# Gated delta-rule decoder step: row spreads and the samples' outer product as one-pass fp32r matmuls with the high and low parts stacked in contraction rows

## What is computed

```python
z = h @ w_in
b_raw, a_raw = z[..., -16:-8], z[..., -8:]                # one value per token and head
beta = sigmoid(b_raw)
g = -exp(a_log) * softplus(a_raw + dt_bias)
o, s_new = _gated_delta_chunked(q, k, v, g, beta, s0)
...
gc = cumsum(chunks(g), axis=-1)
decay = where(tril, exp(gc[..., :, None] - gc[..., None, :]), 0)
lmat = where(strict, einsum('nbhid,nbhjd->nbhij', k * beta, k) * decay, 0)
tinv = triangular_solve(eye + lmat, eye)
u, w = tinv @ (v * beta), tinv @ (k * beta * exp(gc))
# per chunk
v_new = u - w @ s
o = (q * exp(gc)) @ s + (q @ k.T * decay) @ v_new
s = s * exp(gc[-1]) + (k * exp(gc[-1] - gc)).T @ v_new
```

## Time and profile before

| what | value |
|---|---|
| time, median of 3 runs | 1707.37 us (all: 1711.52, 1707.2, 1707.37) |
| span of the profiled execution | 1703.2 us (the page gives no other time of it; it lies 4.2 us under the median) |
| TensorE matmul busy | 1613.1 us, 95% |
| TensorE weight load busy | 1518.8 us, 89% |
| VectorE busy | 850.8 us, 50% |
| ScalarE busy | 515.6 us, 30% |
| GpSimd busy | 219.7 us, 13% |
| mean granted TensorE clock | 0.916 of full |

### The profile page before, as it was taken

One profiled execution on the slowest core, in us unless ns is written; L12 is line 12 of the kernel. 1 busy time (PEld: TensorE's weight loads), 2 busy tenths in 40 slices (PEclk: granted clock), 3 DMA queues, 4 the chain that ended last, 5 costly groups with the idle time before them and its releaser, 6 DMA issues.

```text
span 1703.2 us, 30528 instructions
## 1 busy us (share of the span) xinstructions
PE 1613.1 (95%) x11944; PEld 1518.8 (89%) x11944; DVE 850.8 (50%) x1268; ACT 515.6 (30%) x783; POOL 219.7 (13%) x183
## 2 busy tenths in 40 slices
PE   6999999999999999979999999998879999999998
PEld 5995588999999999978998889887769999999997
DVE  5445512544344334666667666765435443443343
ACT  4122112332122222433343344333224221221234
POOL 5410000200000000213212321231112000000002
PEclk8995555999999999989999999997579999999999
DMA  5345200464355322312122122110022332332322
GB/s 168 87 125 142 56 1 13 124 215 161 116 168 186 98 86 84 90 50 51 40 63 60 42 64 62 51 51 25 27 64 86 90 96 87 91 94 88 94 77 87
DMA packets 229888, 147.25 MB, mean 86 GB/s; under 512 B 5172, under 2 KB 223817, under 8 KB 229412
## 3 DMA queue, kind: packets, MB, share of 16 engines
q1 hardware_dynamic: 227984, 140.63, 28.0%
q0 software_dynamic: 1520, 5.65, 1.1%
q10 hardware_dynamic: 332, 0.24, 0.0%
HBM read 137.31 MB, written 26.36 MB: 96 GB/s over the span
## 4 chain that ended last, share of the span: by engine, by line
PE 84%; DVE 8%; issue 4%; ACT 2%; POOL 1%; DMA 1%; DVEq 0%; SPq 0%; ACTq 0%; POOLq 0%
PE acc L625 53%; PE acc L843 7%; PE aux L934 6%; PE aux L764 2%; PE aux L742 2%; PE aux L916 2%; PE aux L926 2%; DVE y L1704 1%; PE aux L1067 1%; DVE w_lo L1435 1%; PE aux L1040 1%; PE acc L798 1%; PE acc L887 1%; PE acc L797 1%; PE acc L777 1%
## 5 line engine op out<-in xcount | busy, mean ns | idle before, releaser
L1435 DVE TENSOR_TENSOR w_lo<-w_raw,w_hi 128x1024 fp32r<-128x1024 f32 x200 | 265.4, 1327 | 123.9 <-ACT w_hi L1136 117.9
L1136 ACT ACTIVATE w_hi<-w_raw 128x1024 fp32r<-128x1024 f32 x200 | 209.9, 1050 | 231.2 <-PE acc L625 212.2
L625 PE MATMUL acc<-h_hi,w_hi 128*128 128x260 f32 x1664 | 220.2, 284 | 4.8 <-ACT h_hi L1148 4.0
L625 PE MATMUL acc<-h_lo,w_hi 128*128 128x260 f32 x1664 | 218.6, 284 | 0.7 <-DVE h_lo L1442 0.7
L625 PE MATMUL acc<-h_hi,w_lo 128*128 128x260 f32 x1664 | 217.5, 283 | 0.0
L625 PEld LDWEIGHTS acc<-h_hi,w_hi 128*128 128x128 f32 x1664 | 207.6, 189 | 6.8 <-ACT h_hi L1148 5.3
L625 PEld LDWEIGHTS acc<-h_lo,w_hi 128*128 128x128 f32 x1664 | 208.0, 190 | 1.5 <-DVE h_lo L1442 1.5
L625 PEld LDWEIGHTS acc<-h_hi,w_lo 128*128 128x128 f32 x1664 | 207.7, 190 | 0.0
L1928 POOL TENSOR_TENSOR ssum<-ssum,sq 128x520 f32<-128x520 f32 x40 | 56.2, 1404 | 977.4 <-issue 859.9
L625 PE MATMUL acc<-g_hi,w_hi 128*128 128x260 f32 x928 | 125.3, 286 | 8.9 <-ACT g_hi L1175 5.1
L625 PEld LDWEIGHTS acc<-g_hi,w_hi 128*128 128x128 f32 x928 | 117.4, 191 | 11.6 <-ACT g_hi L1175 6.3
(11 more groups left out here) (307 smaller groups left out, 2138.6 us busy)
## 6 DMA issues: line engine op xcount, KB each, us to landing
w_raw<-in_w_ffn_gate SPq DMA_DIRECT2D x44, 512.0 KB, 3.8
w_raw<-in_w_ffn_up SPq DMA_DIRECT2D x44, 512.0 KB, 3.8
w_raw<-in_w_ffn_down SPq DMA_DIRECT2D x32, 512.0 KB, 4.0
w_raw<-in_w_in_c SPq DMA_DIRECT2D x32, 512.0 KB, 4.1
w_raw<-in_w_in_a SPq DMA_DIRECT2D x16, 512.0 KB, 4.0
w_raw<-in_w_ffn_down SPq DMA_DIRECT2D x16, 384.0 KB, 3.3
w_raw<-in_w_out_a SPq DMA_DIRECT2D x8, 512.0 KB, 4.0
s_in<-in_state_gdn SPq DMA_DIRECT2D x8, 512.0 KB, 4.0
```

The source lines that it names most:

```text
L625: last = nc.tensor.matmul(acc[:, 2 * slot + b, 0:TH], w[:, slot, k * P:(k + 1) * P], x[:, k, b * TH:(b + 1) * TH], start=part == 0 and k == 0,
L1136: nc.scalar.activation(w_hi[:, slot], w_raw[:, slot], ACT.Copy).then_inc(w_hi_made, 1)
L1435: nc.vector.tensor_tensor(w_lo[:, slot], w_raw[:, slot], w_hi[:, slot].bitcast(F32), ALU.subtract).then_inc(w_lo_made, 1)
```

## The change

The rows of beta and of the decay stand twice in `rows` (beta at 0 and 32, decay at 64 and 96), and the lower copy of each pair is replaced by what the rounding to fp32r left over. The spreads and the outer product then read fp32r operands, one pass each, and the sum over contraction rows adds high and low parts. For the outer product, k and dv stand in three groups of 8 rows (0, 32, 64), as high, low, high and high, high, low. Line numbers in the rows of order below are those of the program each is of; the diff is cut to its core.

```diff
 delta_table
-    t[0:32, G_HALF:G_HALF + P] = 1.0
-    t[32:64, G_HALF + P:G_HALF + 2 * P] = 1.0
+    t[0:64, G_HALF:G_HALF + P] = 1.0
+    t[64:128, G_HALF + P:G_HALF + 2 * P] = 1.0
-        t[h, G_SEL + h] = t[32 + h, G_SEL + h] = 1.0
+        t[h::32, G_SEL + h] = 1.0
 tiles
-            tokcols = sb("tokcols", [QB, 64], F32, s)
+            rows_r = sb("rows_r", T, F32R, s)
+            half_r = sb("half_r", 2 * P, F32R, s)
+            tokcols = sb("tokcols", [QB, 72], F32, s)
-                rowsel = sb("rowsel", T, F32, s1)
+                rowsel = sb("rowsel", T, F32R, s1)
+                    kv_cols = sb("kv_cols", [2, 96], F32, s2)
-                    dvexp = sb("dvexp", [2, SEQ], F32, s2)
-                    kv_rows = sb("kv_rows", [2, P], F32, s2)
+                    dvexp = sb("dvexp", [2, SEQ], F32R, s2)
+                    kv_rows = sb("kv_rows", [2, P], F32R, s2)
 TensorE, preamble
-                        mm = nc.tensor.matmul(aux[0:64, 2 + b, 0:TH], w[:, k], x[:, k, b * TH:(b + 1) * TH],
+                        mm = nc.tensor.matmul(aux[:, 2 + b, 0:TH], w[:, k], x[:, k, b * TH:(b + 1) * TH],
-                tr = nc.tensor.transpose(aux[:, 2, c * 64:(c + 1) * 64], rows[0:64, c * P:(c + 1) * P], ident[0:64, 0:64])
+                tr = nc.tensor.transpose(aux[:, 2, c * 72:(c + 1) * 72], rows[0:72, c * P:(c + 1) * P], ident[0:72, 0:72])
 TensorE, turn
-                    spread("gc", delta[0:64, G_HALF + P:G_HALF + 2 * P], rowsel[0:64])
+                    spread("gc", half_r[:, P:2 * P], rowsel)
-                    spread("beta", delta[0:64, G_HALF:G_HALF + P], rowsel[0:64])
+                    spread("beta", half_r[:, 0:P], rowsel)
-                    B.done("dk_turned", nc.tensor.transpose(aux[0:NS, 2, P:2 * P], sm[:, 4], ident))
+                    B.done("dk_turned", nc.tensor.transpose(aux[0:72, 2, P:2 * P], kv_cols[:, 0, 0:72], ident))
-                    wait(gb["dve"], "d_rows", hb)
+                    wait(gb["dve"], "dv_lo", hb)
                     for b in range(2):
                         mm = nc.tensor.matmul(auxv(1)[:, b], ones, osq[:, b * TH:(b + 1) * TH], start=True, stop=True)
-                        mm = nc.tensor.matmul(aux[:, 2 + b], kv_rows[0:NS, 0], dvexp[0:NS, b], start=True, stop=True)
+                        mm = nc.tensor.matmul(aux[:, 2 + b], kv_rows[0:72, 0], dvexp[0:72, b], start=True, stop=True)
 VectorE, preamble, between "sum2" and "tokcols" (the steps before work on 40 rows instead of 8)
+            R.done("half_r", nc.vector.tensor_copy(half_r[:], delta[:, G_HALF:G_HALF + 2 * P]))
+            R.done("rows_hi", nc.vector.tensor_copy(rows_r[:], rows[:]))
+            own(R, "rows_hi")
+            for name, part in (("beta_lo", slice(32, 40)), ("cum_lo", slice(96, 104))):
+                R.done(name, nc.vector.tensor_tensor(rows_r[part], rows[part], rows_r[part].bitcast(F32), ALU.subtract))
-            R.done("tokcols", nc.vector.tensor_copy(tokcols[:].rearrange("p c m -> p (c m)"), aux[:, 2, 0:256]))
+            R.done("tokcols", nc.vector.tensor_copy(tokcols[:].rearrange("p c m -> p (c m)"), aux[:, 2, 0:288]))
 VectorE, turn
-                    B.done("dv", nc.vector.tensor_tensor(sm[:, 2], sm[:, 1], sx[:, :, 0], ALU.subtract))
+                    B.done("dv", nc.vector.tensor_tensor(kv_cols[:, 1].rearrange("p (r b) -> p r b", b=32)[:, :, 0:NS], ...
-                    B.done("d_rows", nc.vector.tensor_copy(kv_rows[0:NS].rearrange("p r m -> p (r m)"), aux[0:NS, 2, P:3 * P]))
+                    B.done("d_rows", nc.vector.tensor_copy(kv_rows[0:72].rearrange("p r m -> p (r m)"), aux[0:72, 2, P:3 * P]))
+                    wait(B, "d_rows", hb)
+                    B.done("dk_lo", nc.vector.tensor_tensor(kv_rows[32:40, 0], aux[32:40, 2, P:2 * P], kv_rows[32:40, 0].bitcast(F32), ALU.subtract))
+                    B.done("dv_lo", nc.vector.tensor_tensor(kv_rows[64:72, 1], aux[64:72, 2, 2 * P:3 * P], kv_rows[64:72, 1].bitcast(F32), ALU.subtract))
-                    B.done("dvexp", nc.vector.tensor_tensor(dvexp[0:NS]..., kv_rows[0:NS, 1]..., ident[0:NS, 0:NS]..., ALU.mult))
+                    B.done("dvexp", nc.vector.tensor_tensor(dvexp[0:72]..., kv_rows[0:72, 1]..., delta[0:72, G_SEL:G_SEL + GH]..., ALU.mult))
-                    A.done("keep_k", nc.vector.tensor_copy(sm[:, 4], kn[:, SEQ:T]))
+                    A.done("keep_k", nc.vector.tensor_copy(kv_cols[:, 0].rearrange("p (r b) -> p r b", b=32)[:, :, 0:NS], ...
 GpSimd
-            R.done("wab_pad_b", nc.gpsimd.tensor_copy(wab_pad[:, :, 0:GH], wab_raw[:, :, 0:GH]))
-            R.done("wab_pad_a", nc.gpsimd.tensor_copy(wab_pad[:, :, 32:32 + GH], wab_raw[:, :, GH:2 * GH]))
+            for r in range(2):
+                R.done(f"wab_pad_b{r}", nc.gpsimd.tensor_copy(wab_pad[:, :, 32 * r:32 * r + GH], wab_raw[:, :, 0:GH]))
+                R.done(f"wab_pad_a{r}", nc.gpsimd.tensor_copy(wab_pad[:, :, 64 + 32 * r:64 + 32 * r + GH], wab_raw[:, :, GH:2 * GH]))
+            R.done("kv_zero", nc.gpsimd.memset(kv_cols[:], 0.0))
-                    A.done("rowsel", nc.gpsimd.tensor_tensor(rowsel[0:64], rows[0:64], delta[0:64, ...
+                    A.done("rowsel", nc.gpsimd.tensor_tensor(rowsel[:], rows_r[:].bitcast(F32), delta[:, ...
```

71 lines of the change are left out of this document (38 added, 33 removed).

## The result

| | before | after |
|---|---|---|
| median of the runs, us | 1709.44 (1707.2 to 1716.66, 4 runs, same chip) | 1679.01 (1674.27 to 1681.81, 4 runs) |
| profiled execution: its time, its span | its time not given, 1703.2 | 1674.27, 1672.1 |
| mean granted clock | 0.916 | 0.922 |
| ratio, 95% interval | | 0.9832 [0.9801, 0.9864] |

The change makes the kernel 30.4 us faster by the medians (1.7% by the ratio). The forecast was 18.2 us less than before, 12 us short of that; by its time, 1689.2, it was 10 us too high, and the range's low end, 1680, lies a microsecond above the median measured. That of the changed kernel is the fastest of its four, with the highest granted clock (0.922; the others 0.917 to 0.920), so how many turns lose clock in the others is not seen.

A forecast was written before the change was run, and what follows sets the result against it. TensorE was taken to bound the kernel (84% of the chain). 5.0 + 7.4 + 0.6 + 2.1 - 2.0 = 13.1 us, plus 5.1 of clock, 18.2 off 1707.37: 1689.2 us, range 1680 to 1699.

The forecast's parts named there:

- gc: Spread of gc, 8 times: 0.63 us shorter each, but the gain becomes a wait for egb; counted 0.
- beta: Spread of beta, 8 times: 0.63 us less each, moving the whole chain behind it earlier; 5.0 us gained.
- the outer product: Two one-pass matmuls, 0.67 us instead of 1.91: 1.24 less in each of turns 2 to 7, 7.4 in all.
- The 0.20 ... I leave standing: The excess of a spread's 1.07 us over the 0.87 of an fp32 pair, assumed to stay; otherwise the gain is 0.83.
- Turn 8, 0.6; turn 9, 2.1: Outer product: turn 8 gains a middle value between 0 and 1.24 us; turn 9 gains 2.6 less 0.5 for "osum".
- VectorE, hidden: Low parts dk_lo and dv_lo add 0.5 us per turn on VectorE, hidden by about 1 us of cover: 0.
- rival 2: VectorE becomes what each level waits for, swallowing 8.0 of the 13.1 us: 1699 us; chance 0.15.
- The preamble: Added VectorE work between the scan and turn 0's first piece: 2.0 us lost, bounds 1.6 and 2.6.
- The clock: Falls to the lower clock: 3.4 us from turn 7's outer product and one 1.7 us fall gained, 5.1 in all.
- rival 1: Some turns escape the clock's fall at the long wait for ip: 1683 us, or 1680; chance 0.15.
- Rival 3: The clock falls at a second place in each turn, 3.4 us each, 24 in seven turns: 1718 us; chance 0.05.
- Rival 4: fp32r matmuls with 128 rows of constants or 512 columns are no shorter; only additions remain: 1709 us; chance 0.04.

The follow-up runs named there:

- padded kernel: Changed kernel with the spread of beta issued twelve times instead of once, restoring the old turn length: 1701.84 us, ratio 0.9988 to the kernel before.
- the runs with the move: One VectorE tap of v moved behind the first ip: kernel before 1708.63 us; changed kernel 1673.66; changed kernel with all three products in fp32 1685.04.
- v1: Changed kernel with ScalarE's gcb and egb moved ahead of the last tap of v: 1683.05 us, ratio 0.9876 to the kernel before.

## Why the prediction was right, and where it was not

- **"gc", 0.** Right: in fp32 it makes the turn no longer, and the 0.73 of new wait for `egb` was foreseen as "some 0.6".
- **"beta", 0.63 each, and the outer product, 1.24.** Right to 0.02 us, each by its own run, as long as the product's kind of pass is meant.
- **"The 0.20 ... I leave standing", and "the matmuls with 128 rows beside them have no other price for it".** This step failed. The change has two parts that the prediction took for one: the pass, and the rows. More contraction rows are no cost but a gain, 0.78 us in each turn. The rows that could have told it were there: the pair that takes 0.87, set beside the spread's 1.07 as "of the same form", contracts over 128 rows, the spread over 64; and L969 behind the spread is busy 0.49 where it is 0.38 elsewhere. A turn with a fall became 2.6 us shorter for the 1.9 forecast. From gc to L980 behind beta it is now 0.96 shorter in all (rows included, after the wait), in the rest, around the outer product, 1.68. Up to turn 7's wait for `ip` that is 7 x 0.96 + 5 x 1.68 = 15.1, as found; behind it 1.68 in turn 7, 0.96 - 0.86 and 1.68 - 0.64 in turn 8, -0.65 in turn 9: 2.2, and 1.1 were found, which is within what the split between clock and the rest can tell.
- **Turn 8, 0.6; turn 9, 2.1.** In turn 8 `ip` takes 0.64 of the outer product's gain, as the middle value had it. In turn 9 the product gave 2.5 and "osum" took 0.65 of it: 1.9.
- **VectorE, hidden; rival 2.** Right. From the start of the copy to `kv_rows` it is now 1.08 us to `w_lo` (before: 0.33) and 2.55 to `dvexp` (before: 1.67), so the additions push the queue back by 0.75 to 0.88 (forecast 0.5), with 0.5 us of slack left at `dvexp`; rival 2 was wrong.
- **The preamble, 2.0 lost.** 2.1 for the additions and 2.4 for the whole stretch. `rows_hi` took 0.42 busy, nearer to the 0.4 estimated by the Trainium skill's rule of copies at twice the rate ("VectorE: DVE Perf Modes", "The perf-mode tier table") than to the 0.5 taken; `half_r` 0.29, and the low parts 0.71 each.
- **The clock, 5.1.** Mis-sized, and the larger part of the miss: 12.8 in the turns, of which 10.2 in turns 1 to 7 (18.7 to 8.5, where the prediction had 15.3 and 3.4 before) and 3.0 in turns 8 and 9, which it had left out; 0.5 more was lost at the start of turn 0. Right were the end of the fall in the outer product and that shorter turns shift the places. But three of turns 2 to 7 escape the fall at `ip`, which was rival 1, at 0.15. The time measured, 1679.0, lies nearer to rival 1's 1680 to 1683 than to the forecast. Rival 1's argument for itself (the place shifts) is the one that fits the runs, though none isolates it; the one against it, that it had fallen in all seven turns, was weak evidence, since five of these turns were equally long: the padded kernel, in the execution that was profiled, falls in every turn again at that length.
- **Rival 3, a second fall in each turn.** Not here, but it exists: the kernel before with a shorter wait has a fall behind the outer product in every one of turns 2 to 7 and gives back all that it gained. With the rows of the change it is gone (1.88 us of fp32 over 72 rows, six turns of six without).
- **Rival 4, no shorter pass.** Wrong. The Trainium skill's four passes of fp32 ("FP8 and Floating Point Precision", "TensorE Precision Notes") would give the outer product, by the prediction's estimate, 0.43 and not 0.47; 0.55 to the next start was measured, above both, which tells neither apart.
- 3.4 us of the 31.1 lie ahead of the change and go with this execution, as said below the account. By the medians the gain is 30.4 all the same, so that what makes up for them there was not seen.

What stays open: what sets whether a turn's wait meets a fall. The padded kernel suggests that places in time matter, the runs with the move that the outer product over 8 rows in fp32 brings a fall of its own; they don't say at which turn length the falls would stop, and the shorter turns of v1 (53.72) have more of them than the changed kernel's. So the 9 us of clock that don't come from turn 7's outer product belong to how this kernel happens to lie in time, as far as is known. That 23 to 30 us are lost in turns 8 and 9 and behind turn 7's wait, 7 us apart between two programs that do the same there but for two spreads, was seen, not explained. That the spreads over 128 rows bring 0.2 each and the outer product over 72 the other 0.4 of the 0.78 is read from the starts in the timelines; the spreads were not tried apart from the outer product.

## What to carry to other kernels

Price a change of a matmul's contraction rows apart from its change of precision: short products over few rows, between matmuls over 128, cost time on either side, and a surplus of 0.2 us in a row that nothing owns is a term and not noise. Where one engine gains little at many places, expect part of the gain at the next wait, and look at what stands ahead of the releaser in its own queue; the queue may have two things to be moved and not one. Compare turns at like clock before comparing kernels, and profile more than one execution where a conclusion rests on the clock: here one fall (1.45 us) is worth more than the outer product's shorter pass (1.24), and a kernel that waits less can lose it all to the clock.
